# Hyena transforms: each bank's first and second half of the sums made in turn, and the taps' additions each behind their own subtraction

## The reference, cut to what matters

```python
def hyena_mix(z, n_seg, seg_len, conv_w, conv_b, filt, d_skip):
    u = (short_conv(z, conv_w, n_seg, seg_len) + conv_b).astype(F32)
    v, x1, x2 = jnp.split(u, 3, axis=-1)
    l = u.shape[1]
    filt_f = jnp.fft.rfft(filt, axis=0)
    y = v
    for o, gate in enumerate((x1, x2)):
        conv = jnp.fft.irfft(jnp.fft.rfft(y, n=2 * l, axis=1) * filt_f[None, :, o], n=2 * l, axis=1)[:, :l]
        y = gate * (conv + d_skip[o].astype(F32) * y)
    return y.astype(z.dtype)
```

## The kernel before, in words

| units | what |
|---|---|
| 0 to 3 | Y(0,0) |
| 4 to 9, 10 to 15 | HF of j = 0, then of j = 1, for o = 0 |
| 16 to 19 | Y(0,1) |
| 20 to 25, 26 to 31 | HF of j = 0 and 1 for o = 1 |
| 32 to 35 | four banks of the first transform back (all opened ahead of `back(0, 0)`) |
| 36 to 39, 40 to 43 | Y(1,0), Y(1,1) |
| 44 to 47 | four banks of the second transform back (all opened ahead of `back(1, 0)`) |
| 48 to 51 | transposes of the result |

## Time and profile before

### The profile page before, as it was taken

One profiled execution on the slowest core, in us unless ns is written; L12 is line 12 of the kernel. 1 busy time (PEld: TensorE's weight loads), 2 busy tenths in 40 slices (PEclk: granted clock), 3 DMA queues, 4 the chain that ended last, 5 costly groups with the idle time before them and its releaser, 6 DMA issues.

```text
span 3696.2 us, 48255 instructions
## 1 busy us (share of the span) xinstructions
PE 3569.7 (97%) x19396; PEld 2257.5 (61%) x19396; DVE 1727.0 (47%) x3669; ACT 972.7 (26%) x1822; POOL 630.9 (17%) x572
## 2 busy tenths in 40 slices
PE   6999999989989999999999999999999999999999
PEld 3578976754754444444444588867654568866654
DVE  3877873274752333344334836323531474523531
ACT  5224422222113100000016214213541312312531
POOL 4002320241001312222214013110001102211001
PEclk8999999999999999999999999999999999999999
DMA  6301130463351111111102214120020413310021
GB/s 203 143 10 34 37 109 22 143 203 106 118 205 46 39 41 46 46 46 46 46 25 85 98 58 115 34 72 12 1 92 0 173 36 92 80 61 24 1 86 46
DMA packets 190446, 266.05 MB, mean 72 GB/s; under 512 B 27309, under 2 KB 133401, under 8 KB 189585
## 3 DMA queue, kind: packets, MB, share of 16 engines
q1 hardware_dynamic: 176576, 194.70, 16.9%
q0 software_dynamic: 13648, 68.26, 4.9%
HBM read 228.11 MB, written 34.81 MB: 71 GB/s over the span
## 4 chain that ended last, share of the span: by engine, by line
PE 88%; DVE 6%; ACT 2%; issue 2%; DMA 1%; POOL 0%; POOLq 0%; DVEq 0%; SPq 0%; ACTq 0%
PE ps L3376 19%; PE ps L3247 9%; PE ps L1038 9%; PE ps L4338 7%; PE ps L1060 6%; PE ps L4631 4%; PE ps L4808 3%; PE ps L1125 2%; PE ps L4288 2%; PE ps L4865 2%; PE ps L4848 2%; PE ps L3444 1%; PE ps L1817 1%; PE ps L2938 1%; PE ps L1833 1%
## 5 line engine op out<-in xcount | busy, mean ns | idle before, releaser
L3376 PE MATMUL ps<-big 128*128 128x512 f32 x1624 | 697.1, 592 | 0.0
L3376 PEld LDWEIGHTS ps<-big 128*128 128x128 f32 x1624 | 308.6, 190 | 388.4 <-issue 385.3
L1038 PE MATMUL ps<-big 128*128 128x512 f32 (+1 forms) x1056 | 403.7, 543 | 0.0
L3247 PE MATMUL ps<-big 128*128 128x512 f32 (+1 forms) x896 | 359.3, 562 | 4.2 <-issue 2.1
L1038 PEld LDWEIGHTS ps<-big 128*128 128x128 f32 x1056 | 200.1, 191 | 197.3 <-issue 191.2
L3247 PEld LDWEIGHTS ps<-big 128*128 128x128 f32 x896 | 169.6, 190 | 188.8 <-issue 183.2
L3569 DVE SCALAR_TENSOR_TENSOR big<-ps,big 128x512 f32<-128x512 f32 x212 | 159.1, 750 | 242.7 <-PE ps L3376 208.7
L4338 PE MATMUL ps<-big 128*128 128x256 f32 x1152 | 252.6, 379 | 0.0
L4338 PEld LDWEIGHTS ps<-big 128*128 128x128 f32 x1152 | 217.2, 190 | 29.3 <-issue 0.7
L1060 PE MATMUL ps<-big 128*128 128x256 f32 (+1 forms) x1344 | 229.0, 332 | 0.0
L1060 PEld LDWEIGHTS ps<-big 128*128 128x128 f32 x1344 | 208.0, 191 | 22.2 <-ACT big L2342 2.5
(11 more groups left out here) (516 smaller groups left out, 5244.3 us busy)
## 6 DMA issues: line engine op xcount, KB each, us to landing
big<-in_w_mlp SPq DMA_DIRECT2D x32, 1024.0 KB, 5.4
big<-in_w_in SPq DMA_DIRECT2D x29, 1024.0 KB, 5.5
big<-in_w_mod SPq DMA_DIRECT2D x24, 1024.0 KB, 8.0
big<-in_w_ada SPq DMA_DIRECT2D x24, 1024.0 KB, 6.0
big<-us_scratch SPq DMA_DIRECT2D x72, 256.0 KB, 4.6
hs_scratch<-big POOLq DMA_DIRECT2D x3, 5120.0 KB, 18.6
xs_scratch<-big POOLq DMA_DIRECT2D x16, 640.0 KB, 3.4
big<-hs_scratch POOLq DMA_DIRECT2D x9, 1024.0 KB, 9.1
```

The lines of the kernel that those rows point to most:

```text
L1038: t = e.matmul(b[:, 0:n], wv[:, k, 128 * m:128 * m + 128], K.hT[:, k, t0:t0 + n], start=(k == 0), stop=(k == 7))
L3247: t = e.matmul(b[:, 0:n], wv[:, k, c:c + 128], cat[:, k, t0:t0 + n], start=(k == 0), stop=(k == 7))
L3376: t = e.matmul(z, w[:, k, c], y, start=(first and k == 0), stop=(k == nk - 1), skip_group_check=not first)
```

## The change

In `forward` the two loops change places: for each n, pair 0 and then pair 1. This holds for every caller, so for all transforms of signals and filters of both convolutions. What is released at the last unit stays with the last unit. In `apart` each addition follows the subtraction of its own n at once, behind a wait for all that DVE has issued. No instruction is added or removed on any engine; the number of waits is the same.

```diff
     def forward(self, e, P, what, v, banks, used, ready):
 
-        for pair in range(2):
-            for n, arrays in enumerate(banks):
-                u = ("hyena", what, n, pair)
-                b = self.banks.open(e, u)
-                for half, (cs, odd, src) in enumerate(arrays):
-                    r = 2 * pair + odd
-                    if ready is not None and n == 0:
-                        e.wait_ge(*self.at(*ready, r))
-                    for mt in range(2):
-                        c = 256 * cs + 128 * mt
-                        x = e.matmul(b[:, 256 * half:256 * half + 256], v[:, r, c:c + 128], src[:, 2 * r + mt, :],
-                                     start=(mt == 0), stop=(mt == 1))
-                x.then_inc(P.sem, P.up(("mm", u), *(used if pair and n == len(banks) - 1 else ())))
+        many = range(len(banks))
+        order = [(n, pair) for n in many for pair in range(2)]
+        for n, pair in order:
+            u = ("hyena", what, n, pair)
+            b = self.banks.open(e, u)
+            for half, (cs, odd, src) in enumerate(banks[n]):
+                r = 2 * pair + odd
+                if ready is not None and n == 0:
+                    e.wait_ge(*self.at(*ready, r))
+                for mt in range(2):
+                    c = 256 * cs + 128 * mt
+                    x = e.matmul(b[:, 256 * half:256 * half + 256], v[:, r, c:c + 128], src[:, 2 * r + mt, :],
+                                 start=(mt == 0), stop=(mt == 1))
+            x.then_inc(P.sem, P.up(("mm", u), *(used if pair and n == len(banks) - 1 else ())))
...
     def apart(self, e, V, what, X):
 
         x = X.rearrange("p (c d a) n -> p c d a n", c=2, d=2)
-        us = []
         for cs in range(2):
             u, b = self.second(e, what, cs)
-            us.append((u, b))
             e.tensor_tensor(x[:, cs, 1, cs], x[:, cs, 0, cs], b[:, cs], ALU.subtract).then_inc(V.sem, V.up())
-        for cs, (u, b) in enumerate(us):
-            e.wait_ge(V.sem, V.n - 1)
+            e.wait_ge(V.sem, V.n)
             e.tensor_tensor(x[:, cs, 0], x[:, cs, 0], b, ALU.add).then_inc(V.sem, V.up(("free", u, 0)))
         u, b = self.second(e, what, 2)
         e.tensor_tensor(X[:, 3:7:3, :], X[:, 3:7:3, :], b, ALU.subtract).then_inc(V.sem, V.up(("free", u, 0)))
```

## The result

| | before | changed |
|---|---|---|
| median of nine runs each | 3695.65 us (3692.31 to 3697.41) | 3703.98 us (3700.91 to 3707.86) |
| ratio, 95% interval | | 1.0023 (1.0014 to 1.0032) |
| the profiled execution, its own time | 3698.02 us | 3707.58 us |
| its span | 3696.2 us | 3705.8 us |

The changed kernel is 8.3 us slower, 0.23%.

The account below looks back on a forecast made before the run. PE was taken to bound the kernel, carrying 88% of the chain. Bank wait 3.3, clock 2.2 and second convolution 1.0 made 6.5 us on 3696.0, so 3702.5 us, range 3698.3 to 3706.4.

Parts of the forecast that it names:

- Part 1: First convolution, order in `forward`: unit 17's bank is freed only behind DVE's product (0,0); 4.6 us pause, 3.3 us late.
- Part 2: Clock drop in the work behind the new pause at unit 17: 2.2 us, ends 1.6 and 3.0, 0 without a drop.
- Part 3: Waits inside `apart`: about 0.1 us of DVE each, under 1 us over four calls, cost 0 or inside the 3.3 us.
- Part 4: Second convolution: back(1, 0) waits for a bank freed by signal (1,1)'s first addition, 1.0 us late.
- I keep 1.0, ends 0.5 and 2.6: Size of the late start of back(1, 0): 0.5 if the clock returns as before, 2.6 if its return is put off.
- The rest of the kernel moves as a block: From the next stage's first matmul on, nothing is regained; later work only shifts.
- The likeliest verdict: Whole kernel: a change within 0.2% (7.4 us), near the upper edge; chance 0.65.
- A: The forecast's case: both bank waits and one clock loss, 5.4 to 7.9 us, 3701.4 to 3703.9; chance 0.55.
- rival C: Low clock twice, behind unit 17's pause (3.0 us) and in back(1, 0) (2.6): 8.9 us slower, 3704.9; chance 0.22.

Follow-up runs that it names:

- e4: The changed kernel with ten more matmuls that nothing reads, into bank 7 right ahead of unit 17: 3702.78 us against 3695.17 before, ratio 1.0021.
- e6: The changed kernel with DVE taking taps (0,1) between times and spread of product (0,0): 3693.92 us against 3694.63 before, ratio 1.0001.
- e9: The changed kernel with the new order in the first convolution only, `apart` as changed: 3698.99 us against 3695.34 before, ratio 1.0010.
- e2: The kernel before with the changed `apart` alone, `forward` as before: 3695.63 us, ratio 1.0002.
- e3: The changed kernel with the new order in the second convolution only, `apart` as changed: 3698.29 us against 3695.17 before, ratio 1.0013.
- e12: e11 with six more unread matmuls into bank 7 ahead of back(1, 1): 3685.96 us against 3694.65 before, ratio 0.9979.
- e11: e7 with nine unread matmuls into bank 7 in each of two second-convolution pauses where PE waits for in_w_ada: 3688.43 us against 3695.34 before, ratio 0.9979.
- e1: The changed kernel with `apart` taken back, so the new order in `forward` alone: 3704.21 us against 3695.17 before, ratio 1.0025.
- e5: The changed kernel with the four banks of back(1, 0) opened one by one, each ahead of its own matmuls: 3700.28 us against 3694.63 before, ratio 1.0017.
- e7: The kernel before with times (0,1) ahead of taps (1,0) and (1,1), spread (0,1) behind them: 3689.97 us against 3694.63 before, ratio 0.9986.
- e8: The kernel before with the DVE moves of both e7 and e10: 3689.50 us against 3694.63 before, ratio 0.9987.
- e10: The kernel before with DVE taking taps (0,1) between times and spread of product (0,0): 3694.87 us against 3695.34 before, ratio 0.9999.

## Why the prediction was right

**Part 1, the bank of unit 17: right, and as sized.** 17 units, a pause of 4.53 us (4.6 predicted), ended by an L3064, and 15 units behind. With the clock held at 1.00 (e4) unit 31 is 3.3 us late, as predicted. e6 shows the cause: with the same order and the bank freed early, PE makes all units in one stretch and the 8.3 us are gone.

**Part 2, the clock behind the pause: right, 2.9 us in the profile for 2.2.** It came at the upper end of 1.6 to 3.0. e4 shows it is the standing still. The advice of the Trainium skill against long idle gaps (page "TensorE: Matmul & The Clock Gate", section "Why this matters for your kernels") held behind this pause. Other executions lose less: 1.7 us in e9's profile. For the average execution the size is open, since e4's median shows only 0.7.

**Part 3, `apart`: right.** e2 is the kernel before within 0.1%. The 0.1 us that a wait between two DVE operations costs is in the rows again. The half-size subtraction at 967.71 lasts 0.42 us, and the addition that waits for it starts at 968.16, 0.03 us behind its end and 0.45 behind its start; two subtractions without a wait are 0.32 us apart.

**Part 4, the second convolution: the wait right, the term too small.** The step "I keep 1.0, ends 0.5 and 2.6" is the one that failed in size: that half of the change alone costs 3.1 us (e3; its interval reaches from 0.04% to 0.21%, 1.5 to 7.8 us). The wait was 1.3 us. The prediction looked for the clock's answer only in back(1, 0), which even got 0.5 us shorter. In the profiles of the changed kernel and of e3 low clock came one step later, in back(1, 1), 1.5 and 1.4 us, and at the next stage's start, 1.7 us. "The rest of the kernel moves as a block" left the latter out. Whether the late bank causes these two stays open.

**The sum.** 6.5 predicted, 8.3 measured. The forecast's own case was A, and its 5.4 to 7.9 us miss the result from below; what holds is the wider range and the direction. The changed kernel's profile, 3.3 + 2.9 + 2.5 = 8.7 us in the stage, is nearest to rival C's 8.9, with C's first clock term (3.0) but not its second: back(1, 0) did not stay at low clock longer. By the medians the halves were off in opposite ways, 3.7 us for the first convolution (e9), where parts 1 and 2 say 5.5, and 3.1 for the second, where part 4 says 1.0. Within their intervals that can be chance, but that the sum lies as near as it does is in part luck. The likeliest verdict, "within 0.2%", was missed by 0.03%; the interval of the ratio has both sides of it.

## What to carry to other kernels

In a ring of buffers with two kinds of reader, the order of production sets which reader frees the slot that the producer needs next; number the uses, take them modulo the ring, and ask what each reader has ahead of that release. An order that completes a pair earlier is worth nothing if the consumer starts its long work with the last piece. And a pause of PE costs more than its length: price the clock behind it, and look one or two steps later too, where the clock behind an unchanged wait can be another. A loss of a few microseconds in a single profile may be that alone.

## What was not expected of the hardware

Filling pauses with matmuls that nothing reads kept the granted clock at 1.00 and shortened the work behind by 3.0 us in 29 (e4) and from 10.01 to 7.07 us (e12). It is no sure remedy: e11 and e12 fill the same pause ahead of back(1, 0), and one then takes 7.14 us, the other 8.62.

And the clock's drop does not depend on the length of the pause alone. Behind a 4.53 us pause it cost 2.9 us in one profile and 1.7 in another. Behind the same 2.14 to 2.15 us pause the next stage began at 1.00 in seven of the fourteen profiles and at 0.64 in the other seven, 1.7 us apart. Put side by side, the profiles show a pattern:

| profile | stage, us | back(1, 0), us | back(1, 1), us | clock of the next stage's first 4.69 us |
|---|---|---|---|---|
| before | 139.9 | 9.27 | 8.65 | 1.00 |
| changed | 148.6 | 8.74 | 10.11 | 0.64 |
| e1 | 148.4 | 8.70 | 10.16 | 0.64 |
| e2 | 140.4 | 9.53 | 8.84 | 1.00 |
| e3 | 142.0 | 8.60 | 10.01 | 0.64 |
| e4 | 145.6 | 8.76 | 10.13 | 0.64 |
| e5 | 143.5 | 9.07 | 8.65 | 1.00 |
| e6 | 139.9 | 9.96 | 9.12 | 1.00 |
| e7 | 132.0 | 8.55 | 10.12 | 0.64 |
| e8 | 132.3 | 8.74 | 10.16 | 0.64 |
| e9 | 143.7 | 9.07 | 8.64 | 1.00 |
| e10 | 136.8 | 8.92 | 8.65 | 1.00 |
| e11 | 131.7 | 7.14 | 10.01 | 0.64 |
| e12 | 130.1 | 8.62 | 7.07 | 1.00 |

Wherever back(1, 1) took 10 us or more the next stage began at 0.64, and wherever it took less, at 1.00. With the exception of e12, which fills the pause between them, a back(1, 0) of at most 8.76 us goes with a back(1, 1) of over 10. This bears on part 4. The changed kernel, e1, e3 and e4 have the late bank, and behind it the slow pair, back(1, 1) of over 10 us and the next stage at 0.64; before, e2, e5, e9 and e10 have neither. But e7, e8 and e11 have the slow pair without the late bank, and e6 has the late bank without the slow pair. So the late bank can't be the only cause. When in time these stretches fall may be what decides, which no run here separates.
